# Both rank-96 memory products of a slot behind its score product, and VectorE's order with it

## What is computed

```python
s = jnp.einsum('bhtd,bhsd->bhts', qc, kc) * jnp.exp(d - m_t[..., None])
a = jnp.exp(inter - m_t)
num = a[..., None] * jnp.einsum('bhtd,bhdv->bhtv', qc, C) + jnp.einsum('bhts,bhsv->bhtv', s, vc)
den = a * jnp.einsum('bhtd,bhd->bht', qc, n) + jnp.sum(s, axis=-1)
h = num / jnp.maximum(jnp.abs(den), jnp.exp(-m_t))[..., None]
...
C_new = decay[..., None, None] * C + jnp.einsum('bhsd,bhsv->bhdv', wk, vc)
```

## Time and profile before

| | |
|---|---|
| median of three runs | 3101.23 us |
| the profiled execution: its span, first to last instruction | 3099.1 us |
| PE busy | 2993.6 us, 97% |
| DVE busy | 1686.5 us, 54% |
| ACT busy | 866.9 us, 28% |
| POOL busy | 1078.5 us, 35% |
| granted TensorE clock, mean | 0.989 |

### The profile page before, as it was taken

One profiled execution on the slowest core, in us unless ns is written; L12 is line 12 of the kernel. 1 busy time (PEld: TensorE's weight loads), 2 busy tenths in 40 slices (PEclk: granted clock), 3 DMA queues, 4 the chain that ended last, 5 costly groups with the idle time before them and its releaser, 6 DMA issues.

```text
span 3099.1 us, 50797 instructions
## 1 busy us (share of the span) xinstructions
PE 2993.6 (97%) x19628; PEld 2786.5 (90%) x19628; DVE 1686.5 (54%) x2584; ACT 866.9 (28%) x1542; POOL 1078.5 (35%) x746
## 2 busy tenths in 40 slices
PE   7998899999999999999989999998999999999998
PEld 7885789999999998999967878787998999999997
DVE  5877445544444455444357786878226345444445
ACT  4000542222212224111144444444005122222211
POOL 3232023555555533333201011102332365555553
PEclk9999899999999999999989999999999999999999
DMA  8555211111111113333255655648410111111121
GB/s 228 139 141 141 80 50 42 42 41 54 47 54 47 55 35 119 132 103 104 89 185 193 224 198 198 238 175 294 133 43 28 55 55 41 35 46 48 54 75 57
DMA packets 278260, 319.01 MB, mean 103 GB/s; under 512 B 25909, under 2 KB 217653, under 8 KB 276898
## 3 DMA queue, kind: packets, MB, share of 16 engines
q1 hardware_dynamic: 257777, 250.82, 26.2%
q10 hardware_dynamic: 13048, 40.28, 3.4%
q0 software_dynamic: 7296, 25.96, 2.4%
HBM read 225.68 MB, written 92.19 MB: 103 GB/s over the span
## 4 chain that ended last, share of the span: by engine, by line
PE 79%; DVE 10%; ACT 4%; issue 3%; PEld 1%; DMA 1%; POOL 0%; SPq 0%; another core or an unknown queue 0%; DVEq 0%; ACTq 0%; POOLq 0%; PEldq 0%
PE ps L426 19%; PE ps L427 19%; PE ps L428 19%; PE ps L861 3%; PE ps L860 3%; PE ps L862 3%; PE ps L2404 2%; PE ps L1460 2%; PE ps L1503 1%; DVE CT L1897 1%; PE ps L1469 1%; PE ps L1470 1%; DVE RST L2061 1%; PE ps L1471 1%; DVE HT L2079 1%
## 5 line engine op out<-in xcount | busy, mean ns | idle before, releaser
L426 PE MATMUL ps<-AH,WH 128*128 128x352 f32 x3072 | 999.1, 325 | 5.0 <-POOL WL L413 2.0
L428 PE MATMUL ps<-AH,WL 128*128 128x352 f32 x3072 | 985.2, 321 | 0.0
L427 PE MATMUL ps<-AL,WH 128*128 128x352 f32 x3072 | 985.2, 321 | 0.0
L426 PEld LDWEIGHTS ps<-AH,WH 128*128 128x128 f32 x3072 | 576.7, 188 | 30.3 <-issue 23.9
L427 PEld LDWEIGHTS ps<-AL,WH 128*128 128x128 f32 x3072 | 577.8, 188 | 1.1 <-issue 0.2
L428 PEld LDWEIGHTS ps<-AH,WL 128*128 128x128 f32 x3072 | 576.9, 188 | 0.0
L411 POOL TENSOR_SCALAR WH<-RAW 128x1024 fp32r<-128x1024 f32 x152 | 180.3, 1186 | 953.0 <-PEq L433 752.6
L413 POOL TENSOR_TENSOR WL<-RAW,WH 128x1024 fp32r<-128x1024 f32 x152 | 400.7, 2636 | 12.7
L1084 DVE TENSOR_TENSOR X<-X,ps 128x352 f32<-128x352 f32 x432 | 225.2, 521 | 264.4 <-PE ps L862 134.0
L975 ACT ACTIVATE SGF<-ps 128x352 f32<-128x352 f32 x192 | 88.7, 462 | 680.0 <-PE ps L428 679.8
L1036 DVE TENSOR_TENSOR HR<-SGF 128x352 f32<-128x352 f32 x144 | 92.8, 644 | 288.4 <-ACT SGF L975 286.5
(11 more groups left out here) (355 smaller groups left out, 5097.0 us busy)
## 6 DMA issues: line engine op xcount, KB each, us to landing
RAW<-in_ffn_w SPq DMA_DIRECT2D x128, 512.0 KB, 3.8
CT<-in_state_mlstm_C SPq DMA_DIRECT2D x32, 1024.0 KB, 5.5
out_C_s<-CT SPq DMA_DIRECT2D x32, 1024.0 KB, 6.0
RAW<-in_ml_w_in SPq DMA_DIRECT2D x32, 512.0 KB, 3.9
RAW<-in_conv_w_pw SPq DMA_DIRECT2D x24, 512.0 KB, 8.1
STK<-u_scratch SPq DMA_DIRECT2D x64, 184.0 KB, 3.9
xc_scratch<-XC ACTq DMA_DIRECT2D x16, 528.0 KB, 2.7
so_scratch<-SO ACTq DMA_DIRECT2D x16, 528.0 KB, 3.7
```

Of the source, the lines that this page charges most:

```text
L426: pe.matmul(ps[:, bank, 0:CW], wh[:, k, cols], hi[:, k, cs], start=(k == 0), stop=False)
L427: pe.matmul(ps[:, bank, 0:CW], wh[:, k, cols], lo[:, k, cs], start=False, stop=False)
L428: mm = pe.matmul(ps[:, bank, 0:CW], wl[:, k, cols], hi[:, k, cs], start=False, stop=(k == nk - 1))
```

## The change

The order of the instructions changes on two engines; their number and their operands don't.

```diff
@@ phase_b_pe
                 if m:
                     if m[1] == 0:
                         old_memory(m[0])
-                    new_memory(m[0], 2 * m[1])
                 if q + 2 < NS:
                     scores(q + 2)
                 if q == LAST[1]:
                     denominators(1, q)
                 if m:
+                    new_memory(m[0], 2 * m[1])
                     new_memory(m[0], 2 * m[1] + 1)
@@ phase_b_dve
-                if m:
-                    update(m[0], 2 * m[1])
                 if q + 2 < NS:
                     weighted(q + 2)
                 for tc in range(3):
                     if q == LAST[tc] + 1:
                         sum_tiles(dve, h, tc, 1)
                 if m:
-                    update(m[0], 2 * m[1] + 1)
+                    update(m[0], 2 * m[1])
                 if q + 2 < NS:
                     add_weighted(q + 2)
                     low(q + 2)
+                if m:
+                    update(m[0], 2 * m[1] + 1)
```

## The result

The changed kernel takes 3110.78 us (median of 8 runs, 3107.74 to 3113.03) against 3101.05 us for the kernel before (8 runs). The ratio is 1.003, 95% interval 1.0021 to 1.0039: **9.7 us slower**, clear of noise, and more than the 0.2% (6.2 us) that the prediction took as the least that tells from no change. The forecast was 3105.8, +4.6 us, with a chance of 0.59 for within 0.2%; the time lies at the upper end of its range (3111). The profiled execution has a span of 3107.2 us, 8.1 us above the one before.

A forecast was written before the change was run, and what follows sets the result against it. Bounds taking turns: PE's own work and a chain through VectorE and ScalarE. PE's order adds zero, three heads 3.9 us, the last head 0.7: 3101.2 + 4.6 = 3105.8 us, range 3098 to 3111.

The forecast's parts named there:

- PE's neighbours cost nothing: PE's own order: even slots stay at 3.29 us and odd slots at 2.20, so no gain or loss.
- The mechanism: VectorE's slots: weighted's idle time holds no update, both updates follow, and skip, gate and centre come 0.65 us later.
- No shift up to slot 6: Slots 2 to 6: no shift taken at normalise(0), the first values of tile 1 or weighted(8).
- The middle is paid back: Slots 6 to 14: PE runs about 0.5 us late, then recovers; weighted(16) stays within 0.1 us.
- the forecast's 0.6: Slot 14, heads 0 to 2: two updates between weighted and the block weights make these 0.6 us later.
- Slot 17, +1.6 on top of what arrives, 0.3 absorbed: Heads 0 to 2: values of slot 17 start 1.6 us later, 0.3 is absorbed at the denominators, leaving +1.3 per head.
- The last head +0.7: Last head: weighted(18) stays, gate is 0.65 us later, and PE waits through GpSimd's store and split: +0.7 us.
- SyncE's queue has slack: SyncE's stores of the memories start about 1 us later, but PE waits for no load of them: no cost.
- the middle isn't paid back: Rival: waits at second products of slots 8, 11, 12 add 0.5 to 0.8 us per head; 3109.2 us, chance 0.28.
- The forecast's own case: Whole kernel: +4.6 us, to 3105.8 us; the case between +2 and +6 us had a chance of 0.45.

The follow-up runs named there:

- e9: The changed kernel with VectorE's order weighted, update, update, add, low (second update back ahead of add and low): 3109.03 us, ratio 1.0022, +7.3 us against before.
- e10: The changed kernel with VectorE's order update, weighted, add, low, update (first update back ahead of weighted in every slot): 3116.44 us, ratio 1.0051, +14.7 us against before.

## Why the prediction was right and wrong

- *PE's neighbours cost nothing*: right. Slot 4 measures 3.29 us as computed. The old memory's start to the scores' start was to be about 1.1 and is 0.99, still above the 0.95 below which the prediction would have called itself wrong. The scores' weight load isn't hidden; in the changed kernel it starts with its product:

```profile
1799.26 1.59 PEld L1503 LDWEIGHTS ps<-QT,XCH 128*128 128x128 f32 x8 [0.84 <-issue]
```

  The page "TensorE: Matmul & The Clock Gate" of the Trainium skill (Step-by-step: what each phase is for), as the prediction applied it, would have hidden the scores' weight load behind the old memory. The 0.84 us of idle time and the unchanged 3.29 us show no such gain here.
- *The mechanism*, both updates behind weighted's wait, skip and gate 0.65 later: right, in its place and size (skip stands 0.66 behind the start of the second update). The places where it should bite were named, slots 8, 11, 12 and 17, and each of them did in head 1. Slot 11 isn't in PE's list above, since there it's the product's weight load that waits, 0.53 us; the pair of products takes 1.03 us (1836.16 to 1837.19) instead of 0.65.
- *No shift up to slot 6*: wrong by 0.36 us. In slot 5 weighted stands right behind inverse and waits 0.32 us for DT, which the first update used to fill, and normalise comes 0.37 later. The values of slot 6 waited 1.49 us in place of 1.25.
- *The middle is paid back*: this is the step that failed. PE was to meet scores(16) unmoved. Its record starts 0.40 late and is shown 0.10 early, so it is 0.50. Slot 8 cost 1.20 instead of 0.5: 0.36 came from slot 5, and 0.38 from gate, which took 1.60 us instead of 1.22. The values of slot 14 are still 0.73 late (1851.95 - 1850.08 - 1.14), and the scores' new place in the slot takes off 0.24. The prediction counted the 0.49 us that weighted(16) waits as room. It isn't: weighted waits there for PE's own scores. It still waits 0.45 after the change, and every bit of PE's lateness passes through it. VectorE passes the rest straight on:

```profile
1851.44 0.42 DVE L1905 TENSOR_TENSOR PT<-ps,DT 128x256 f32<-128x256 f32 x1 [0.45 <-PE ps L1503]
...
1853.77 1.89 DVE L1999 TENSOR_TENSOR BD<-WROW,bdm 128x512 f32<-128x512 f32 x3
```

  Against the earlier trace rows and the 1.14: weighted +0.50, block weights +1.16. The 0.66 between the two is the forecast's 0.6; the 0.50 is the middle.
- *Slot 17, +1.6 on top of what arrives, 0.3 absorbed*: right in size. 0.50 arrives, and 2.34 - 0.50 = 1.8. The next head's queries are 0.37 less late than that. In the last head no product waits in slot 17.
- *The last head +0.7*: 1.44 was measured up to its last denominators, and the path was wrong. Weighted(18) was to stay; counted from the head's first denominators it comes 0.95 later, 0.50 from the middle and 0.45 from slot 15. There weighted stands behind inverse and waits 0.26 us for DT, as in slot 5. The second update adds the rest, to 1.4. GpSimd's store, too, is 1.6 later (2157.45 against 2150.32, less 5.53), but PE's wait of 3.5 us for GpSimd's split isn't there any more. In the changed kernel PE waits 3.1 us for a sum of VectorE's instead.

  Beside it stands a wait that wasn't in the sum. The old memory of slot 16 waited 0.63 us for the load of the last memory.

```profile
PE ps L1536 <- DMA CT<-in_state_mlstm_C: 0.6, 1, 0.6
```

  The prediction said that SyncE's queue has slack and that the stores start about 1 us later. SyncE issued this load at 2130.69 in the kernel before and at 2140.70 in the changed one, 4.5 us later within the head. The load must wait until the store out of the same buffer has landed. That store was issued 2.1 us later, and the load came 8.64 us behind it instead of 6.23:

```profile
2132.06 0.37 SPq L1331 DMA_DIRECT2D out_C_s<-CT  x1
2140.70 0.38 SPq L1291 DMA_DIRECT2D CT<-in_state_mlstm_C  x1
```

  The wait probably cost little in the end. The update that the second product of slot 17 needs ended at 2154.31, and PE reached that product at about 2154.44 (2154.20 and 0.24 for the first of the pair).

So the result is the rival "the middle isn't paid back", put at 3109.2 us with a chance of 0.28: its point of decision (PE over 0.5 late at scores(16)) was just reached, and the carried part plus slot 17 gave 2.1 us in heads 0 and 1, where that rival computed 2.0. Its reason was another one: VectorE's waiting wasn't used up, it had never been room. The forecast's own case had the right sign and half the size. The time is inside the range only because the range took this rival in.

## What to carry to other kernels

When a consumer's instructions are reordered to follow a producer's new order, ask of each one what it used to fill: an instruction that is ready ahead of one that waits is free there, and behind it delays all that follows by up to its full length, whatever the wait is for. When you look for room downstream, ask for whom each wait is: a wait for the engine that you have just made late is no room. Do the order slot by slot rather than by one rule for all, since the first update ahead of weighted gained when done in six slots (-2.4 us) and lost when done in all (+8.5 us). And look at who makes the waited-for operand late: moving ScalarE's DT ahead of its own idle time was worth more than either order.

## What the runs showed of the hardware

**TensorE's clock fell behind two waits beside each other, in one head of four.** In the changed kernel the granted clock fell once within the heads, behind the waits of slot 8 in head 2 (stretch, its length, PE busy, granted clock, DMA share, GB/s):

```profile
1968.00:1972.00 4.00, 2.98 (x14) 0.70 0.69 266
1972.00:1976.00 4.00, 4.00 (x33) 0.88 0.73 242
```

PE had stood idle for 0.76 and then for 1.02 us just before. The value products there start 0.64 us apart per group of three instead of 0.36, near the lower of the two levels (1.2 against 2.4 GHz):

```profile
1970.96 0.41 PE L1517 MATMUL ps<-PH,VH 128*128 128x256 f32 x1
1971.60 0.42 PE L1517 MATMUL ps<-PH,VH 128*128 128x256 f32 x1
```

By the old memory of slot 10 head 2 is 1.6 us behind its sister heads; 0.5 us of it is left at the end, since the later waits take the rest in. The kernel before, the one with all six slots refilled and the one with refill in slots 5 and 6 have no such stretch between 1640 and 2152 us. VectorE's order alone has three, and the changed kernel with early DT has three as well, from 1676, 1820 and 1996 us on. The refill in slots 9 and 10 has one, TensorE's order alone two, e9 two and e10 four. That can be a price of the waits that no sum of their lengths has. That the waits are its cause is read from where it falls, and wasn't tried by itself. They aren't enough for it: heads 0, 1 and 3 of the changed kernel and all heads of the one with refill in 15 and 16 have the same waits in slot 8 and keep the clock.

**VectorE and GpSimd slow each other in turn.** GpSimd's masking, in the kernel before and then in the changed one:

```profile
1816.01 1.62 POOL L1372 TENSOR_SCALAR VM<-VS,BM 96x512 fp32r<-96x512 f32 x1 [10.28 <-PE ps L1563]
```

```profile
1817.51 1.03 POOL L1372 TENSOR_SCALAR VM<-VS,BM 96x512 fp32r<-96x512 f32 x1 [10.52 <-PE ps L1563]
```

Most of its 32 records last 0.69 us. Before, it started 0.16 us behind gate (1815.85), ran beside gate and `center` and took 1.62 us, and gate took 1.22. After, it had run for 0.50 us when gate started (1818.01); it took 1.03, and gate 1.60. All five gates of the changed kernel that start while a masking runs take 1.60 us, the other ones of these heads 1.22. So of gate and masking the one that starts second is slowed. Alone, masking takes 0.69 us; 1.62 is 0.93 more, near the 0.98 of gate that was left (to 1816.99). `center`, which started at 1816.99 while masking ran and reads PSUM, kept its 1.21. Why that is wasn't tried.
